# FFN pairs 3 to 10 on a plain 384-column input, a 2 MB table loaded in pieces, and two U gatings back to back

## The reference, cut to what matters

```python
def adaln_input(h, mod, j, g):
    return rms_norm(h, g) * (1 + mod[:, :, 3 * j + 1]) + mod[:, :, 3 * j]

def swiglu(x, w_gu, w_down):                      # w_gu 1024 x 5632, w_down 2816 x 1024
    gate, up = jnp.split(x @ w_gu, 2, axis=-1)
    return (jax.nn.silu(gate) * up) @ w_down
# for both layers i, twice (ffn1, ffn2), with h = 384 x 1024:
#   h = h + 0.5 * adaln_gate(m, j) * swiglu(adaln_input(h, m, j, norm_g[i, j]), w_gu, w_down)

def sgu_mixer(xn, w_in, v_g, w_s, b_s, w_out):
    u, v = jnp.split(jax.nn.gelu(xn @ w_in, approximate=False), 2, axis=-1)
    v = rms_norm(v, v_g)
    vg = v.reshape(B, nc, SGU_CHUNK, SGU_GROUPS, gw)
    sv = jnp.einsum('gts,bcsgd->bctgd', w_s, vg) + b_s.T[None, None, :, :, None]
    gated = u.reshape(B, nc, SGU_CHUNK, SGU_GROUPS, gw) * sv
    return gated.reshape(B, S, SGU_WIDTH) @ w_out
```

## Time and profile before

| | us |
|---|---|
| median of 3 runs | 1580.26 (1578.96 to 1581.96) |
| profiled execution, its own time | 1584.25 |
| its span, first to last instruction | 1582.4 |
| PE busy in it | 1538.7 (97%) |
| DVE, ACT busy | 1119.8 (71%), 594.8 (38%) |
| mean granted TensorE clock | 0.990 |

### The profile page before, as it was taken

How to read it: one execution, slowest core, us unless ns; L and a number is a source line. 1 busy time by engine, 2 the same in 40 slices (tenths; PEclk the granted TensorE clock), 3 DMA queues, 4 the chain that set the end, 5 groups by cost and what they waited for, 6 DMA issues and landing times.

```text
span 1582.4 us, 23595 instructions
## 1 busy us (share of the span) xinstructions
PE 1538.7 (97%) x9159; PEld 1509.4 (95%) x9159; DVE 1119.8 (71%) x1521; ACT 594.8 (38%) x840; POOL 74.0 (5%) x59
## 2 busy tenths in 40 slices
PE   6999999989989999999999999999999999999999
PEld 6899999989848999999999999999999999999999
DVE  6768787968896887887877878887846355454423
ACT  3333332254474533332253333225643244333321
POOL 2000000013100200000020000002000010000000
PEclk9999999989999999999999999999999999999999
DMA  9265545734223355455634555663542432333332
GB/s 386 83 228 185 200 177 209 264 115 173 95 71 134 107 186 202 170 209 219 248 120 162 204 193 182 238 244 112 208 160 81 160 106 107 127 112 133 124 117 92
DMA packets 49647, 262.70 MB, mean 166 GB/s; under 512 B 6704, under 2 KB 7984, under 8 KB 27568
## 3 DMA queue, kind: packets, MB, share of 16 engines
q1 hardware_dynamic: 49584, 261.82, 45.1%
HBM read 259.57 MB, written 2.23 MB: 165 GB/s over the span
## 4 chain that ended last, share of the span: by engine, by line
PE 85%; DVE 5%; issue 3%; ACT 3%; DMA 2%; SPq 1%; POOL 1%; DVEq 0%; ACTq 0%; POOLq 0%
PE ps L1209 25%; PE ps L1210 25%; PE ps L1211 25%; PE ps L1243 2%; PE ps L1244 2%; PE ps L1246 2%; ACT w_hi L523 1%; DVE mprod L789 1%; DMA raw_x<-panels 1%; PE ps L1428 1%; DVE x_lo L852 1%; PE ps L1521 1%; DVE w_lo L781 1%; DMA raw<-panels 1%; DVE h L936 1%
## 5 line engine op out<-in xcount | busy, mean ns | idle before, releaser
L523 ACT ACTIVATE w_hi<-raw 128x2048 fp32r<-128x2048 f32 x164 | 314.4, 1917 | 665.1 <-PE ps L1211 563.1
L1209 PE MATMUL ps<-x_hi,w_hi 128*128 128x386 f32 (+1 forms) x1520 | 519.8, 342 | 13.1 <-DVE x_lo L852 8.7
L781 DVE TENSOR_TENSOR w_lo<-raw,w_hi 128x2048 fp32r<-128x2048 f32 x163 | 373.2, 2290 | 214.5 <-ACT w_hi L523 213.5
L1210 PE MATMUL ps<-x_lo,w_hi 128*128 128x386 f32 (+1 forms) x1520 | 518.2, 341 | 0.0
L1211 PE MATMUL ps<-x_hi,w_lo 128*128 128x386 f32 (+1 forms) x1520 | 516.7, 340 | 0.0
L789 DVE SCALAR_TENSOR_TENSOR mprod<-mraw,cB 128x1024 f32<-128x1024 f32 x256 | 313.1, 1223 | 7.4
L1209 PEld LDWEIGHTS ps<-x_hi,w_hi 128*128 128x128 f32 x1520 | 288.0, 189 | 16.7 <-issue 7.3
L1210 PEld LDWEIGHTS ps<-x_lo,w_hi 128*128 128x128 f32 x1520 | 288.6, 190 | 0.7
L1211 PEld LDWEIGHTS ps<-x_hi,w_lo 128*128 128x128 f32 x1520 | 287.9, 189 | 0.0
L1209 PE MATMUL ps<-act_hi,w_hi 128*128 (+1 forms) x832 | 279.6, 336 | 1.5 <-DVE act_lo L1196 1.5
L1211 PE MATMUL ps<-act_hi,w_lo 128*128 (+1 forms) x832 | 279.6, 336 | 0.0
(11 more groups left out here) (149 smaller groups left out, 1156.9 us busy)
## 6 DMA issues: line engine op xcount, KB each, us to landing
raw<-panels SPq DMA_DIRECT2D x164, 1024.0 KB, 5.2
mraw<-mod_rows SPq DMA_DIRECT2D x128, 512.0 KB, 3.5
raw_x<-panels SPq DMA_DIRECT2D x5, 1024.0 KB, 6.0
mshift<-mod_rows SPq DMA_DIRECT2D x8, 512.0 KB, 15.5
mscale<-mod_scale SPq DMA_DIRECT2D x6, 512.0 KB, 12.2
bias<-na_bias SPq DMA_DIRECT2D x1, 2048.0 KB, 8.1
h<-x_in_t SPq DMA_DIRECT2D x1, 1536.0 KB, 11.0
out<-h SPq DMA_DIRECT2D x4, 384.0 KB, 2.3
```

Of the source, the lines that this page charges most:

```text
L523: nc.scalar.activation(w_hi[q0 % 2][:, :], raw[q0 % 2][:, :], ACT.Copy).then_inc(hi_done, 1)
L781: nc.vector.tensor_tensor(w_lo[q0 % 2][:, :], raw[q0 % 2][:, :], w_hi[q0 % 2][:, :].bitcast(F32), ALU.subtract).then_inc(lo_done, 1)
L1209: mm(out, w[0][:, cols], xs[0], start=start, stop=False)
L1210: mm(out, w[0][:, cols], xs[1], start=False, stop=False)
```

## The change

- **Plain input.** In pair 0 and 1 of each FFN, DVE and ACT make `x2_hi`, `x2_lo` [128, 8, 384]: for each of 8 feature blocks `h * sqsum` (DVE, `scale_x2`), scale and shift (ACT, `shifted`, two instructions), rounded copy (ACT), subtraction (DVE, `low_x2`). Pairs 3 to 10 read these with 384 columns. Their Silu is one ACT instruction from PSUM, their product with up one DVE instruction from PSUM; L892, the four Silu, L902 and the four L907 are gone there. `x2` lies where `raw_x`, `hi_x`, `lo_x` lie. The loop is pairs 3 to 10 on all engines.
- **Modulation blocks.** Blocks start in pair 2 of FFN 0 (9 of them) and in pair 3 of FFNs 1 and 2 (8 each); down 0 has 9, V has 6, and the SGU's output panels have 2.
- **Tables.** The position table comes with the mask already in it, in four loads of 512 KB beside QKV; the seven small loads stand behind the third down panel of FFN 0; the mask's addition is gone.
- **Spare panel** of FFN 2 is loaded when PE has finished FFN 1's up panels.
- **SGU end.** DVE does two products, then the panel split, then two subtractions. The order of turns is the same.

```diff
-MOD_GU = GU - 1
-MOD_DN = (8, 8, 8)
-MOD_IN, MOD_OUT, MOD_SG = 4, 2, 4
-MOD_AT = (8, 32, 50)
+MOD_AT = (8, 32, 48)
+MOD_FROM = (2, 3, 3)
+MOD_DN = (9, 8, 8)
+MOD_IN, MOD_OUT, MOD_SG, MOD_OUT1 = 4, 2, 6, 2
...
+            x2_hi = sb("x2_hi", [P, KD, T], F32R, scope=s)
+            x2_lo = sb("x2_lo", [P, KD, T], F32R, scope=s)
...
-                sp.wait_ge(spare_pe, 1)
-                sp.dma_start(bias[:, :, :, :], na_bias).then_inc(bias_in, 16)
+                sp.wait_ge(pe_done, down_panel(0))
...
+            def shifted(f, k):
+                base = (NORM_OF[f] // 3 * NMOD + 3 * (NORM_OF[f] % 3)) * KD
+                act.wait_ge(x2_scaled, KD * f + k + 1)
+                for cond, cols in ((0, CTX), (1, LAT)):
+                    last = nc.scalar.activation(sq[:, k % 4, cols], sq[:, k % 4, cols], ACT.Identity,
+                                                bias=modT[:, base + k, cond:cond + 1], scale=aT[:, k, cond:cond + 1])
+                last.then_inc(x2_shifted, 1)
+                act.wait_ge(x2_shifted, KD * f + k + 1)
+                nc.scalar.activation(x2_hi[:, k, :], sq[:, k % 4, :], ACT.Copy).then_inc(x2h_done, 1)
...
+                    else:
+                        act.wait_ge(pe_done, gate_panel(f, g0) + 1 + 2 * ii)
+                        act.wait_ge(actl_done, done)
+                        last = nc.scalar.activation(tmp[:, 0:2, 0:T], ps[:, gate_bank(g0):gate_bank(g0) + 2, 0:T], ACT.Silu)
                     last.then_inc(silu_done, 1)
+                    if g0 == 1:
+                        for k in range(4):
+                            shifted(f, k)
                     split(up_panel(f, g0) + 2, ii)
                     act.wait_ge(mul_done, done + 1)
                     nc.scalar.activation(act_hi[:, bass.ds(2 * g0 + 2 * ii, 2), :], tmp[:, 0:2, 0:T], ACT.Copy) \
                         .then_inc(acth_done, 1)
+                    if g0 == 1:
+                        for k in range(4, KD):
+                            shifted(f, k)
...
+                def scale_x2(k):
+                    nc.vector.tensor_tensor(sq[:, k % 4, :], h[:, k, :], sqsum[:, 0:T], ALU.mult).then_inc(x2_scaled, 1)
+                def low_x2(k):
+                    dve.wait_ge(x2h_done, KD * f + k + 1)
+                    nc.vector.tensor_tensor(x2_lo[:, k, :], sq[:, k % 4, :], x2_hi[:, k, :].bitcast(F32), ALU.subtract) \
+                        .then_inc(x2_done, 1)
+                def plain_pair(g0, ii, b, done):
+                    split(gate_panel(f, g0) + 2, ii)
+                    if b is not None:
+                        mod_sum(b, ii)
+                        mod_out(b, ii)
+                    dve.wait_ge(pe_done, up_panel(f, g0) + 1 + 2 * ii)
+                    dve.wait_ge(silu_done, done + 1)
+                    nc.vector.tensor_tensor(tmp[:, 0:2, 0:T], ps[:, up_bank(g0):up_bank(g0) + 2, 0:T], tmp[:, 0:2, 0:T],
+                                            ALU.mult).then_inc(mul_done, 1)
                     split(up_panel(f, g0) + 2, ii)
+                    low_act(g0, ii, done)
...
+                    if g0 >= 3:
+                        done = PAIRS[f] + g0 + ii
+                        pe.wait_ge(x2_done, KD * (f + 1))
+                        pe.wait_ge(silu_done, done - 1)
+                        project(feature_major, gate_panel(f, g0), ii, gate_bank(g0), T, (x2_hi, x2_lo))
+                        pe.wait_ge(mul_done, done - 1)
+                        project(feature_major, up_panel(f, g0), ii, up_bank(g0), T, (x2_hi, x2_lo))
                         return
```

More of the change, by code:

```diff
@@ L277, in build, with loop_pairs @@
         dve_steps = [0]
-        def loop_pairs(f, eng, pair, straight=1, first=0):
-            block = lambda g: MOD_AT[f] + g - 1 if f < 3 and g else None
+        def loop_pairs(f, eng, pair, straight=3, first=0):
+            block = lambda g: MOD_AT[f] + g - MOD_FROM[f] if f < 3 and g >= MOD_FROM[f] else None
             for g in range(first, straight):
@@ L354, in mod_block, with down @@
                         .then_inc(mraw_in[a], 16)
-            def down(q0, n, block=0, blocks=0, spare=lambda: None):
+            def down(q0, n, block=0, blocks=0, between=()):
                 def step(j0, i, beside):
@@ L363, in down @@
                 step(1, 0, False)
-                step(2, 0, blocks > 0)
-                spare()
-                steps_beside_blocks(sp, 3, max(0, blocks - 1), n, step)
+                for j, load in enumerate(between):
+                    step(2 + j, 0, j < blocks)
+                    load()
+                steps_beside_blocks(sp, 2 + len(between), max(0, blocks - len(between)), n, step)
             def spare_panel(f):
@@ L464, in _ @@
                 panel(Q_U + g, 0)
-            down(Q_OUT1, KS // 2, spare=spare_behind_gate)
+            down(Q_OUT1, KS // 2, MOD_V + MOD_SG, MOD_OUT1, [spare_behind_gate])
             gate_up(3)
@@ L1226, in mod_scale_tile, with feature_major @@
                 last.then_inc(mod_pe, 1)
-            def feature_major(q0, bank, order, w=T):
+            def feature_major(q0, bank, order, w=T, xs=(x_hi, x_lo)):
                 for a, k in order:
                     last = three(ps[:, bank + a, 0:w], slot(q0), slice(256 * k + P * a, 256 * k + P * a + P),
-                                 (x_hi[:, k, 0:w], x_lo[:, k, 0:w]), k == 0, k == KD - 1)
+                                 (xs[0][:, k, 0:w], xs[1][:, k, 0:w]), k == 0, k == KD - 1)
                 return last
@@ L1600, in band @@
     dc = col[None, :] - col[:, None] + 15
-    ok = (dc >= 0) & (dc <= 30)
-    t = rpb[:, dr][..., np.where(ok, dc, 0)]
-    t = np.where(ok, t, np.float32(0))
+    first = np.clip(col - 8, 0, GRID - 16)[:, None]
+    inside = (col[None, :] >= first) & (col[None, :] < first + 16)
+    t = rpb[:, dr][..., np.where(inside, dc, 0)]
+    t = np.where(inside, t, np.float32(-1e30))
     return t.transpose(1, 3, 0, 2, 4).reshape(2, P, NH, NLAT).transpose(1, 0, 2, 3)
@@ L1661, in shape_constants @@
             rope[1, :, at] = np.sin(ang) * (1 if b else -1)
-    qcol = (np.arange(P) % GRID)[:, None]
-    start = np.clip(qcol - 8, 0, GRID - 16)
-    kcol = np.arange(GRID)[None, :]
-    mask = np.where((kcol >= start) & (kcol < start + 16), 0.0, -1e30).astype(np.float32)
-    return rope, mask
+    return rope
 def kernel(**inputs):
```

163 lines of the change are left out of this document (96 added, 67 removed).

## The result

The changed kernel took 1565.81 us (median of four runs, 1564.60 to 1569.92) and the kernel before, beside it on the same chip, 1579.61 (1578.47 to 1581.96): a ratio of 0.9909 with an interval of 0.9893 to 0.9925, 13.8 us less. Forecast were 1562.5 and 17.7 less. Run once more as a control it took 1563.83 against 1580.4, ratio 0.989 (0.9871 to 0.9909), 16.6 less. So the forecast was right in sign and lay within its range; the first measurement missed its sum by 3.9 us.

The account below looks back on a forecast made before the run. PE, busy 1538.7 of 1582.4 us, was taken as the bound. Terms 11.9 + 4.8 + 1.5 - 0.5 = 17.7 off the median 1580.26 gave 1562.5 us; the forecast's own range was 1560 to 1565, the whole range 1559.5 to 1573.

Parts of the forecast that it names:

- Plain input, 11.9: FFN pairs 3 to 10: 64 panels go from 8.506 to 8.32 us, a gain of 11.9 us.
- the layout: Projection matmuls: rows of 1544 bytes against 1536, not the two columns, make most of the 3.9 ns.
- a multiple of 64 bytes: Projections: a row of act_hi is 1536 bytes, a multiple of 64; x2 gets the same, x has 1544.
- The x2 chain, 0: Pairs 0 and 1: the added DVE and ACT work fits, 1.6 us to spare; rival that it doesn't, chance 0.07.
- FFN 0, 0.5 lost: FFN 0's pairs: a modulation block in pair 2 delays up 3 and pairs 4 and 5; 0.5 us, 0 to 2.
- Table, 4.8: FFN 0, about 98 us: 3.2 us of PE waiting and 1.6 of lower clock go; gain 3.2 to 4.8.
- the 1.6 us: FFN 0, 102 to 112 us: the lower clock after PE's wait costs about 1.6 us, which go too.
- SGU's end, 1.5: End of the SGU: PE's wait for the seventh act_lo goes, 1.5 us gained, from 0 to 1.5.
- Down 0's tail, 0 (0 to 0.6): End of down 0: mask's 4.48 us go, a block of 5.3 and gain scalings of 0.3 come; cost 0.
- the loop as a rival: FFN pairs: gate loads wait behind mraw loads, which wait for DVE's sums; 29 us, 1591, slower; chance 0.04.

Follow-up runs that it names:

- act shifted: The changed kernel with act_hi and act_lo 128 bytes further on in memory, nothing else moved: 1565.69 us, ratio 0.9902.
- the padded x: The changed kernel with rows of x_hi and x_lo 392 columns apart: 1566.02 us, ratio 0.99.
- the short block: The changed kernel with the sums of down 0's ninth block taken over 64 of 1024 inputs, loads as before: 1562.1 us, ratio 0.9884.
- the extra loads: The changed kernel with one extra 256 KB load ahead of each panel's load in down 0, panels 3 to 10: 1564.78 us, ratio 0.9914.
- the new load order: The changed kernel with each FFN raw load issued ahead of the two mraw loads before it: 1562.02 us, ratio 0.9882; again 1562.43, 0.9894.

## Why the prediction was right, and where its sum was not

- **Plain input, 11.9.** Right: 0.186 us on each of 64 panels, 8.506 to 8.32. The reason given was at best half right. It named the layout for most of the 3.9 ns a matmul. With rows of 386 under 384 columns 0.11 of 0.186 us come back, so 7 of the 11.9 us, and the two columns are 5. That the row distance is how is not shown, since the down panels slowed in the same run without it, and in the run with act shifted the same panels took 8.32 and 8.48 within one execution. The explanation by a multiple of 64 bytes was not tested, and that the new panels would get exactly the down panels' number was a choice that came out, not a thing derived. The Trainium skill's page "TensorE: Matmul & The Clock Gate" ("Back-to-back issue gap") sets the spacing by the matmul's columns and the weight load; the run with x2 rows of 386 disagrees, for both panels have 384 columns and the same weight loads, and 8.43 is not 8.32.
- **The x2 chain, 0.** Right in FFNs 1 to 3, whose panels tick at 8.32 from pair 3 on, and FFN 2 as a whole gained the 2.98 of its panels.
- **FFN 0, 0.5 lost.** FFN 0's projections gained 7.10; 5.00 of it is the table by the run with that part alone, and 2.98 would be the 16 panels. So 0.9 us were lost there, within 0 to 2, at pair 5 and not at pair 3. In the control trace nearly nothing was: the projections took 167.56, and 167.54 to 167.56 in the traces with the padded x, the short block, the extra loads and act shifted. So as a rule nothing is lost there, and the 0.9 belong to one execution.
- **Table, 4.8.** 5.0 measured, in one trace of that part alone. The clock stays at 1.00 where the wait is gone, so it was right to count the 1.6 us.
- **SGU's end, 1.5.** 1.7 measured, in the changed kernel and alone.
- **Down 0's tail, 0 (0 to 0.6).** This is the term that was mis-sized: 3.7 us in the profiled execution. 2.0 of it is PE's wait for squares of h, 1.7 the norm's lower clock (8.6 us instead of 7.0 for the same 32 matmuls). The working compared one sum, 4.48 of mask against 5.3 of block, and took DVE's place before it as given. But the ninth block is not just longer than the mask: it needs two more mraw loads and a panel's turn in the loop, and it takes the one split of down 0 that had no block behind it, in which DVE could catch up. The mask had one merit, that nothing was loaded behind it. The prediction had the loop as a rival, for the pairs, and argued that late turns don't follow each other; in down 0 they do, with eight blocks as with nine. What it costs differs between executions: in the control trace PE loses 0.3 us of waiting there instead of 2.0.

Together: 11.9 + 5.0 + 1.7 - 0.9 - 3.7 = 14.0, against 14.3 between the spans. This accounts for the profiled execution, the slowest of its four; that the median fell 3.9 us short of the sum for the same reason is likely and not shown, since the other three have no trace. Without the tail it is 17.7 to 18, which the traces without a gap show: the kernel with the new load order has a span of 1560.0, and the one with only the SGU part, whose start is equally undisturbed, 1575.8. Between them lie 15.8 us, and with the 1.7 that the SGU part has already taken it is 17.5.

The best version is the changed kernel with the raw loads ahead. Its waits in down 0 are gone in both traces; its medians are 1.4 to 3.8 us under those of the changed kernel, in different groups and with intervals that overlap, so that gain is shown by the traces and only likely by the times.

## What to carry to other kernels

When work is added to an engine beside loads that wait for that same engine, follow the ring (load, copy, subtraction, sums, next load) and count its slack per turn, 0.7 us of 8.3 here; a ring makes up no more than that slack a turn, so late landings pile up (1.2, 2.3 and 3.4 us late at 266.78, 284.47 and 302.22) unless a turn without the extra work comes. Issue the load that the critical path needs before the one that waits for slack work: here that gave 12.2 us in hand instead of 7.4 at no cost. And a term of the sum that compares only durations ("4.5 leaves, 5.3 comes") should also ask what each of the two waits for.

## What the runs showed that I had not expected

- The spacing of matmuls with equal columns is not one number: 384 columns took 8.32 us a panel on rows of 1536 bytes, 8.43 on rows of 1544 in x2, 8.47 in x, 8.41 on rows of 1568. It repeats to 0.01 us from panel to panel. But down panels, on rows of 1536, took 8.48 in one kernel; moving them by the same 128 bytes alone gave 8.32, and in two traces the last panels of down 0 went from 8.32 to 8.48 behind one late matmul. The edits move the number, but layout alone doesn't fix it. What does is open.
- The same kernel's executions differ by fixed pieces: the 8 us before pair 1 of FFN 0 ran at a granted clock of 0.65 or at 1.00, some 3 us apart, and attention at 0.92 or 1.00, 2.5 us apart. Two traces must be compared stage by stage before a difference of 3 us is put down to a change.
- The norm behind down 0 took 7 to 9 us for 32 matmuls. All four traces with eight blocks there have 7.0; with nine it was 7.0 to 9.2, with and without a gap in front (8.2 with none). What lowers the clock there was not tried.
